# Low parts of the weights formed in four pieces, with the consumer waiting piece by piece, and two bank waits split in two

## The reference, cut to what matters

```python
# first block
h = rms_norm(x, g); proj = h @ w_in          # 15 tiles needed at once, 16 gate tiles needed late
y_pool = pooling_mixer(u) @ w_pool_out       # running sums over 2, 4, 8, 16 tokens
y_nsa  = nsa_mixer(q, k, v, ...) @ w_nsa_out # compressed blocks + two kinds of attention
x = x + (gate_pool * y_pool + gate_nsa * y_nsa) @ w_out
x = x + (silu(conv(gate)) * val) @ w_down    # gate, val = split(rms_norm(x) @ w_up)
# second block
qkv = silu(causal_conv(h @ w_in_2[...]))     # then a chunked gated delta rule (a triangular inverse)
ob  = chunk_band_attention(...)
x = x + (sig(ga) * (oa @ w_branch_a) + sig(gb) * (ob @ w_branch_b)) @ w_out_2
x = x + (silu(gate) * up) @ w_down_2         # gate, up = split(conv(rms_norm(x) @ w_up_2))
```

## Time and profile before

| | us |
|---|---|
| median of 3 runs | 1627.44 (1626.38 to 1628.12) |
| the profiled execution, its own time | 1629.67 |
| its span, first to last instruction | 1627.9 |
| PE busy | 1550.2 (95%) |
| DVE busy | 919.4 (56%) |
| ACT busy | 570.8 (35%) |
| POOL busy | 180.8 (11%), 92 instructions |

### The profile page before, as it was taken

How to read it: one execution, slowest core, us unless ns; L and a number is a source line. 1 busy time by engine, 2 the same in 40 slices (tenths; PEclk the granted TensorE clock), 3 DMA queues, 4 the chain that set the end, 5 groups by cost and what they waited for, 6 DMA issues and landing times.

```text
span 1627.9 us, 21109 instructions
## 1 busy us (share of the span) xinstructions
PE 1550.2 (95%) x7702; PEld 1233.0 (76%) x7702; DVE 919.4 (56%) x1430; ACT 570.8 (35%) x872; POOL 180.8 (11%) x92
## 2 busy tenths in 40 slices
PE   5998899899999999999999989989999999999997
PEld 4876666688888888888777668766788877877885
DVE  5139565465666666333763562337566787787323
ACT  5134355543433333222324413235544223223221
POOL 2437111100000000000001243132100000000000
PEclk9999899999999999999999999999999999999998
DMA  6322111252322223222222241162242222223221
GB/s 223 142 104 97 58 59 40 72 181 91 104 90 91 103 103 105 93 102 75 91 101 89 93 128 66 46 220 104 84 151 96 97 90 90 103 90 110 92 104 70
DMA packets 57090, 164.77 MB, mean 101 GB/s; under 512 B 11696, under 2 KB 11960, under 8 KB 56896
## 3 DMA queue, kind: packets, MB, share of 16 engines
q1 hardware_dynamic: 51616, 157.67, 27.6%
q10 hardware_dynamic: 5408, 6.21, 1.2%
HBM read 148.89 MB, written 14.96 MB: 101 GB/s over the span
## 4 chain that ended last, share of the span: by engine, by line
PE 80%; DVE 10%; ACT 4%; issue 3%; POOL 1%; DMA 0%; ACTq 0%; DVEq 0%
PE banks L1576 24%; PE banks L1578 23%; PE banks L1577 23%; PE banks L1667 2%; PE banks L1697 2%; ACT at_p L844 1%; PE banks L1678 1%; ACT at_pt L853 1%; DVE at_sm L1186 1%; DVE w_lo L543 1%; POOL w_lo L543 1%; DVE cols L1190 1%; DVE t_raw L1086 1%; DVE pool_pad L511 1%; PE banks L1958 0%
## 5 line engine op out<-in xcount | busy, mean ns | idle before, releaser
L1576 PE MATMUL banks<-h_hi,w_hi 128*128 128x512 f32 x1312 | 533.4, 407 | 31.9 <-POOL w_lo L543 20.7
L1578 PE MATMUL banks<-h_hi,w_lo 128*128 128x512 f32 x1312 | 514.3, 392 | 0.0
L1577 PE MATMUL banks<-h_lo,w_hi 128*128 128x512 f32 x1312 | 513.6, 391 | 0.0
L743 ACT ACTIVATE w_hi<-w_raw 128x1024 fp32r<-128x1024 f32 (+1 forms) x228 | 251.5, 1103 | 474.4 <-PE banks L1578 414.8
L1576 PEld LDWEIGHTS banks<-h_hi,w_hi 128*128 128x128 f32 x1312 | 248.1, 189 | 105.6 <-issue 26.7
L1578 PEld LDWEIGHTS banks<-h_hi,w_lo 128*128 128x128 f32 x1312 | 247.7, 189 | 53.6
L1577 PEld LDWEIGHTS banks<-h_lo,w_hi 128*128 128x128 f32 x1312 | 248.2, 189 | 52.6 <-issue 5.1
L543 DVE TENSOR_TENSOR w_lo<-w_raw,w_hi 128x1024 fp32r<-128x1024 f32 (+1 forms) x167 | 216.6, 1297 | 78.9 <-ACT w_hi L743 78.9
L543 POOL TENSOR_TENSOR w_lo<-w_raw,w_hi 128x1024 fp32r<-128x1024 f32 x61 | 148.4, 2433 | 434.2 <-ACT w_hi L743 434.1
L1576 PE MATMUL banks<-act_hi,w_hi 128*128 128x512 f32 x352 | 137.2, 390 | 1.6 <-DVE t_raw L1086 0.8
L1578 PE MATMUL banks<-act_hi,w_lo 128*128 128x512 f32 x352 | 137.0, 389 | 0.0
(11 more groups left out here) (285 smaller groups left out, 1777.3 us busy)
## 6 DMA issues: line engine op xcount, KB each, us to landing
w_raw<-in_w_up SPq DMA_DIRECT2D x88, 512.0 KB, 3.5
w_raw<-in_w_fill SPq DMA_DIRECT2D x44, 512.0 KB, 3.5
w_raw<-in_w_down SPq DMA_DIRECT2D x32, 704.0 KB, 3.9
late_scratch<-stage SPq DMA_DIRECT2D x44, 256.0 KB, 2.1
w_raw<-in_w_mix SPq DMA_DIRECT2D x16, 512.0 KB, 4.3
sg<-late_scratch SPq DMA_DIRECT2D x16, 512.0 KB, 3.8
w_raw<-in_w_out SPq DMA_DIRECT2D x16, 512.0 KB, 3.5
w_raw<-in_w_in SPq DMA_DIRECT2D x15, 512.0 KB, 3.5
```

The source lines that it names most:

```text
L743: act.activation(w_hi[:, c.slot, 0:kt * P], w_raw[:, c.slot, 0:kt * P], ACT.Copy)\
L1576: pe.matmul(dst, w_h, hi[:, kr, :], start=first and n == 0, stop=False)
L1577: pe.matmul(dst, w_h, lo[:, kr, :], start=False, stop=False)
L1578: mm = pe.matmul(dst, w_l, hi[:, kr, :], start=False, stop=last and n == len(ks) - 1)
```

## The change

The low parts that POOL makes are formed in four instructions of 256 elements a partition in place of one of 1024 (`low_pieces`), each incrementing `lo_ready`. The semaphore therefore counts four to a chunk; the low parts of DVE, still one instruction, add 4. All waits on it are scaled (`lows`): loads, the dense stages and the merges still wait for the whole chunk. Only the filling on TensorE waits at each of its four steps for the piece that this step reads. The waits on the two banks behind `ffn` and behind in2c are moved into the next stage, where the first tile waits for the read of the first bank alone and the second tile for that of the second bank.

```diff
+    def lows(self, more=0):
+        return lin(PIECES * (self.first + more), 2 * PIECES * self.half, self.i)
...
             eng.tensor_tensor(w_lo[:, c.slot, 0:kt * P], w_raw[:, c.slot, 0:kt * P],
-                              w_hi[:, c.slot, 0:kt * P], ALU.subtract).then_inc(lo_ready, 1)
+                              w_hi[:, c.slot, 0:kt * P], ALU.subtract).then_inc(lo_ready, PIECES)
+
+        def low_pieces(eng, c):
+
+            eng.wait_ge(hi_ready, c.count(1))
+            for r in range(PIECES):
+                cols = slice(2 * r * P, 2 * (r + 1) * P)
+                eng.tensor_tensor(w_lo[:, c.slot, cols], w_raw[:, c.slot, cols], w_hi[:, c.slot, cols],
+                                  ALU.subtract).then_inc(lo_ready, 1)
...
             def load(c, name, kt):
-                wait(sp, lo_ready, c.count(-1))
+                wait(sp, lo_ready, c.lows(-1))
...
-            low(pool, Chunk(0, 0, 0, None, False), DK)
-            low(pool, Chunk(1, 0, 0, None, False), DK)
+            low_pieces(pool, Chunk(0, 0, 0, None, False))
+            low_pieces(pool, Chunk(1, 0, 0, None, False))
             for i, j in units(pool, INFO["in1"][0]):
-                next_low(pool, "in1", i, j)
+                next_low(pool, "in1", i, j, 0, True)
...
                         c = chunk(name, n // 2, n % 2)
+                        pe.wait_ge(lo_ready, c.lows() + r + 1)
                         if r == 0:
-                            pe.wait_ge(lo_ready, c.count(1))
                             if n < 2:
...
-            def linear(name, n, used, per=1, mean=True):
+            def linear(name, n, used, per=1, mean=True, banks_free=None):
...
-                    pe.wait_ge(lo_ready, c.count(1))
+                    pe.wait_ge(lo_ready, c.lows(1))
+                    if banks_free and isinstance(i, int) and i == 0:
+                        pe.wait_ge(banks_free[0], banks_free[1 + j])
...
-                pe.wait_ge(conv_done[b], steps * (FK - 1) + 5)
+
+            def ffn_banks(b, steps):
+                return conv_done[b], steps * (FK - 1) + 1, steps * (FK - 1) + 5
...
-            residual("down1", 2, act_hi, act_lo, act_hl[0])
+            residual("down1", 2, act_hi, act_lo, act_hl[0], ffn_banks(0, 5))
...
-            pe.wait_ge(cv_done, 5 * 11 + 1)
-            linear("in2z", 2, copied["in2z"], mean=False)
+            linear("in2z", 2, copied["in2z"], mean=False, banks_free=(cv_done, 5 * 10 + 1, 5 * 11 + 1))
...
-            residual("down2", 4, act_hi, act_lo, act_hl[1])
+            residual("down2", 4, act_hi, act_lo, act_hl[1], ffn_banks(1, 8))
```

More of the change, by code:

```diff
@@ L543, in low, with next_low @@
             eng.tensor_tensor(w_lo[:, c.slot, 0:kt * P], w_raw[:, c.slot, 0:kt * P],
-                              w_hi[:, c.slot, 0:kt * P], ALU.subtract).then_inc(lo_ready, 1)
-        def next_low(eng, name, i, j, q=0):
+                              w_hi[:, c.slot, 0:kt * P], ALU.subtract).then_inc(lo_ready, PIECES)
[5 more added lines that the diff above has]
+                                  ALU.subtract).then_inc(lo_ready, 1)
+        def next_low(eng, name, i, j, q=0, pieces=False):
             c2, kt2 = ahead(chunk(name, i, j, q), INFO[name][2])
-            if c2:
+            if c2 and pieces:
+                low_pieces(eng, c2)
+            elif c2:
                 low(eng, c2, kt2)
@@ L671, in serve @@
                     while state[0] < upto:
-                        next_low(pool, name, state[0] // 2, state[0] % 2)
+                        next_low(pool, name, state[0] // 2, state[0] % 2, 0, True)
                         state[0] += 1
                 return serve
-            low(pool, Chunk(0, 0, 0, None, False), DK)
-            low(pool, Chunk(1, 0, 0, None, False), DK)
+            low_pieces(pool, Chunk(0, 0, 0, None, False))
+            low_pieces(pool, Chunk(1, 0, 0, None, False))
             for i, j in units(pool, INFO["in1"][0]):
-                next_low(pool, "in1", i, j)
+                next_low(pool, "in1", i, j, 0, True)
             pool.wait_ge(copied["in1"], 15)
@@ L703, in _ @@
             pool.memset(gb_rows[:, :], 0.0).then_inc(blk_zero, 1)
-            pool.wait_ge(lo_ready, BASE["fill2"] + 2)
+            pool.wait_ge(lo_ready, PIECES * (BASE["fill2"] + 2))
             serve = lows("fill2", FILL2, FILLED2)
@@ L1120, in merge @@
             def merge(name, b, sg, mt, mix_hi, mix_lo):
-                dve.wait_ge(lo_ready, BASE[name] + 2)
+                dve.wait_ge(lo_ready, PIECES * (BASE[name] + 2))
                 for i, j in units(dve, DK):
@@ L1624, in linear, with residual @@
                         norm(n)
-            def residual(name, n, hi, lo, split_):
+            def residual(name, n, hi, lo, split_, banks_free=None):
                 nchunk, kt = INFO[name][1], INFO[name][2]
```

## The result

The changed kernel takes 1602.14 us (median of 4 runs, 1600.24 to 1604.65) against 1627.78 for the kernel before beside it (4 runs, 1626.38 to 1628.14): ratio 0.9846, 95% interval 0.9833 to 0.9858, so 23 to 27 us faster. The forecast was 1612 with a range of 1604 to 1622. The direction was right, the size too small by 10 us, and the time fell 2 us outside the range, where rival (d) had put it.

What follows compares the result with a forecast made beforehand. TensorE, busy 95% of the span, was taken as the bound, through its waits and lower-clock time. Terms 3.1 + 3.8 + 5.4 + 1.3 + 4.0 - 0.3 = 17.3 us, less a tenth 15.5: 1627.44 - 15.5 = 1612, range 1604 to 1622.

Steps and rivals of the forecast that it cites:

- rival (d): Pieces let DVE through everywhere, the lower clock at 974 and 162 goes too: 24 to 26 us, 1602; chance 0.10.
- Part 1: Bank waits at three stage borders: each costs nothing once moved, 3.1 us gained, bounds 2.3 to 3.2.
- Part 2: TensorE's direct waits for low parts in fill2: the first piece comes 1.7 us earlier, 3.8 us gained, bounds 2.4 to 4.3.
- Part 3: Around the inverse, 939 to 977 us: DVE's chain earlier, shorter waits, half the clock loss: 5.4 us, bounds 1.7 to 8.
- part 4: First mixers, 144 to 164 us: DVE's copy done earlier, clearing then meets a `tensor_scalar`: 1.3 us, bounds -0.4 to 4.6.
- the tenth taken off: Off the whole sum of 17.3 us, because a chain made earlier meets the next engine, leaving 15.5.
- Part 5: Attention 1 and 2: small `tensor_scalar` instructions before the exponentials get through earlier, 4.0 us, bounds -0.5 to 7.
- Part 6: Costs: in1 hides the longer low parts, the start loses 0.3 us, 132 more waits in the filling cost zero.
- Rival (a): GpSimd keeps the shared port from piece to piece: 8.0 us gained, 1619.4; chance 0.24.
- Rival (b): A piece has a large fixed cost, 1.25 us each: 10 us slower, 1637; chance 0.04.
- Rival (c): Only the bank waits gain, since TensorE next waits for DVE or ScalarE at the same places: 3.1 us, 1624.3; chance 0.07.

Runs made afterwards that it cites:

- the second experiment: The changed kernel with GpSimd's four pieces, but the filling waits at its first step for the whole chunk; ratio 0.9921 to the kernel before.
- the first experiment: The changed kernel with each GpSimd low part as one instruction again, split bank waits and 132 added waits kept; ratio 0.9968 to the kernel before.
- the kernel with both orders: The kernel before, with VectorE's copy ordered ahead of the low part of turn 2 and the clearing behind the low parts of compress 4; ratio 0.9963.

## Why the prediction was right in direction and short in size

Part 1 was right: 3.1 forecast, 3.0 in the trace. Part 2 was right in its sum, 3.8 against 4.0; that a filling must not wait for the last piece was in it only as "the first ends 1.7 earlier", and the second experiment prices that at 12 us.

Part 3 was a little low, 5.4 against 6.6. VectorE's chain got through as forecast (2.05 and 1.24 at 958.43 and 965.26), and the stretch at the lower clock went whole, 1.55, where half was counted. It is not safe: in the changed kernel with the clearing late the clock was granted at 0.50 from 951.60 to 954.90 again. One sign was missed here: 2.6 us of waits for low parts were left outside the start, where at most 1.5 had been announced.

The step that failed is in part 4: "the clearing then meets a `tensor_scalar` of the next sum, and the four pieces take turns with sums that need the same port", hence 1.3 of the 4.6. In the changed kernel VectorE is ahead by the time it gets here: its copy stands at 141.08, before the low part at 141.67, and the `tensor_scalar` is over before the clearing begins. The clearing caught the second copy alone, for 1.7. The lines, VectorE and then GpSimd of the changed kernel:

```profile
141.08 0.42 DVE L512 COPY pool_pad<-p 128x512 f32<-128x512 f32 x1
...
144.55 0.84 DVE L518 TENSOR_SCALAR pool_pad<-pool_pad 128x496 f32<-128x496 f32 x1
...
147.63 2.10 DVE L512 COPY pool_pad<-p 128x512 f32<-128x512 f32 x1
```
```profile
141.67 4.31 POOL L554 TENSOR_TENSOR w_lo<-w_raw,w_hi 128x256 fp32r<-128x256 f32 x4 [0.66 <-ACT w_hi L756]
...
145.93 3.52 POOL L707 MEMSET pc_t<- 128x4096 f32 x1
```

That gave 5.4, 4.1 over the forecast: 4.2 where TensorE waits (4.65 and 1.62 before, 2.40 now, each with its restart), where 1.3 was forecast, and 1.3 of matmuls that ran at the lower clock before and not now, where nothing was. It is 4 of the 10 us missed; the others are the tenth taken off (1.7), parts 3 and 5 (1.2 each) and what the start gave beyond mix2 and the end (1.2). The forecast kept every instruction at its old time and let only the stall change: the mechanism was right, and the step that failed is the size of this term, with the collision priced into it. The collision it foresaw does happen, with two pieces and with the copy ordered first; which victim the clearing finds depends on shifts of a few tenths. Upper bounds of 4.6 and 2 had been written beside the 1.3, and the range did not make room for them.

Part 5 was 1.2 low (4.0 against 5.2). In the shape of the earlier trace rows at 220.03 (2.18) VectorE's small `tensor_scalar` beside pieces took 0.51, 0.26 and 0.75, where it took 2.18, 1.90 and 2.40 before:

```profile
212.17 0.51 DVE L1203 TENSOR_SCALAR cols<-cols 128x4 f32<-128x4 f32 x1
...
226.49 0.26 DVE L1203 TENSOR_SCALAR cols<-cols 128x2 f32<-128x2 f32 x1
...
245.32 0.75 DVE L1203 TENSOR_SCALAR cols<-cols 128x4 f32<-128x4 f32 x1
```

TensorE started 1.65, 0.80 and 1.63 earlier behind these three, 4.1 for the 3.5 that part 5 had counted in attention 1. The rest is clock, which part 5 did not have: 1.4 won behind 260.94, 0.7 lost again near 193, where a stretch at the lower clock is new. In the changed kernel the third instruction stood behind one piece alone (0.75), as forecast; that the kernels with whole low parts won the same 3.07 us by order means only that taking the pieces away there does not lose it.

Part 6 put costs of 0.3 and was right that in1 hides the rest (whole low parts there change nothing, -0.6) and that the waits are free. The 2.85 at the start are for the most part not the change's: 0.9 is an earlier first transfer, 1.4 the lower clock at 32. Nearly as much is lost again in mix2 (1.4, a new stretch at the lower clock) and at the end.

"I take off a tenth" failed too: 1.7 us for chains that meet the next engine. No such loss is in the table, whose -1.9 at mix2 and the end is for the most part clock; the terms added up. The gains by stage, -0.6, 7.8 and 10.4, with 5.2 for the kernel without pieces, make 22.8 against 25.1.

Rival (a), GpSimd keeping the port from piece to piece, is refuted by every contested row. The doubt came from the copy at 144.75, which did not get in between a low part and the clearing; that was seen again in two further profiles, and still VectorE gets its turn between pieces. Why the clearing goes ahead of the waiting copy there stays open. Rival (b) fell by the 0.70 of a piece. Rival (c) is what the first experiment built: 5.2, not 25. Rival (d) came true in size and mostly in mechanism: through at the port everywhere, the lower clock at 974 gone and that at 162 cut from 10.2 to 3.4 us; that new stretches came near 193 and in mix2 it had not.

## What to carry to other kernels

Where two engines share a port, read their timelines side by side and look for the longest instruction that stands in a chain, a clearing as much as arithmetic: moving one 3.52 us clearing into idle time gave the kernel before 5.2 us, a fifth of what the whole change gave, and the changed kernel 1.9, which can't be told from nothing. Cut a long instruction of the side engine into pieces only together with a consumer that waits piece by piece; with a wait for the last piece half of the gain was lost, in fill2 all of it. A gain that the trace shows is not yet what its cause is worth: 3.07 us in attention 1 stayed when the pieces were taken out, by the order of two requests. When a shift makes a chain earlier, replay it with the new times before pricing the next collision, and give the range the bound that was written beside a term.

## What the runs showed of the hardware

GpSimd and VectorE take turns at the end of each instruction when both want the shared port: 1.13 us for a sum that takes 0.69 alone, less than the 1.39 of a sum and a piece one after the other. An exception is the copy of 6.12, which the clearing overtook. Pieces of half the size gave no more that could be told (26.4 against 25.1). Two requests within 0.04 us fall one way in one kernel and the other way in the next: 0.03 behind gave 6.12 and 6.10 (three executions), 0.04 ahead gave 0.42, and with the clearing moved 0.02 behind gave 0.42 as well. The `tensor_scalar` in attention 1 took 2.39 to 2.40 when some 0.01 behind a whole low part (six executions) and 0.17 when some 0.05 ahead of it (three).

A clearing held VectorE's copy (2.10) and `tensor_scalar` (3.15), but not sums of two operands: in the kernel with the copy first the clearing ran from 146.44 to 149.96, and three sums from 143.55, the last of them inside it, took 4.22, as they did with no clearing near them (4.23, in the kernel with both orders), while the `tensor_scalar` at 147.81 took 2.43. The Trainium skill, SBUF — State Buffer, section Who interferes with whom, says that a VectorE instruction with two SBUF inputs contends with a GpSimd one that reads SBUF, not with one that only writes it, and that copies and `tensor_scalar` can take the whole pair; these rows agree. It adds that whoever issues first gets the ports; by the recorded starts that held in most rows, and failed in the one of 0.02 us. It has the loser stand for the whole instruction of the other, and there the 1.13 us, under 1.39, decides. The prediction had told the rule for two inputs in SBUF without the exception for an instruction that only writes.
